# One layer of a hybrid encoder on one core: the mLSTM as one masked decay matrix per head, rotary by partition shuffles, query heads in pairs, gates as scans of rows

## The chip, the cores and the metric

One Trainium2 chip, one of its cores. The metric is the device time of one execution in microseconds, the median over several runs.

## The reference

One layer for a prompt of 256 tokens and a sample of 64 tokens, which share all weights; the kernel treats both as T = 320 columns. Everything reads xn = RMSNorm(x) through one input projection:

```python
# A: mLSTM, 8 heads of 128, chunk by chunk of 64 tokens
b = cumsum(lf);  logD = where(causal, b_t - b_s + ig_s, -inf)
m_t = max(b + m, max_s logD);  D = exp(logD - m_t);  inter = exp(b + m - m_t)
S = (q @ k.T) * D
h = (S @ v + inter * (C @ q)) / max(|sum(S) + inter * (n @ q)|, exp(-m_t))
C, n = decayed C, n + weighted outer products          # returned too
# B: 8 index heads of 64 with one key, relu, weighted sum, top-k keys per query;
#    softmax attention of 8 query heads (2 key/value heads of 128) over these keys;
#    q, k, index q, index k rotated in their first quarter of dimensions
# C: attention of 4 heads of 256 to 256 memory tokens
merged = sum_b sigmoid(G_b(xn)) * P_b(branch_b);  h = x + merged @ w_out
y = RMSNorm(h + ConvFFN(RMSNorm(h)))
```

## The kernel before, in words

Every product with weights is cut into **tiles** of 128 output features by 320 token columns (256 for the memory tokens). A tile has two **units** of eight k-blocks. In float32r, three products make one (high·high, low·high, high·low; `multiply`, L546 to L548), so a tile is 48 matmuls into one of two alternating PSUM banks `G`. SP loads a unit (512 KB) into one of four raw slots; ACT's `split` (L972) casts it to `w_hi`, DVE's `split` (L1333) subtracts that into `w_lo`, two units ahead of PE. After a tile ACT or DVE reads its bank, and PE may do a **stage** of small fp32 work into the six banks `M`: transposes by the identity (`turn`, L559) and products (`mm`, L562). The order on each engine is written out by hand in program order; the engines are tied by semaphores alone.

The order of the stages is C (4 heads of 6 tiles), B (10 tiles), A (8 heads of 4 tiles q, k, v, o), Q (8 query tiles), then gates and branches, output projection, FFN. What the change touches:

- **B and head 0 of A.** B's tiles are v, v, the gates i and f, the index key with the index weights, four of index queries, two of keys. For the rotary PE multiplies by a rotation matrix (the `mm` on `rin`, and `q_rotate` in Q) and DVE does three passes (`rope`, L1466). The gates are turned to tokens on rows; PE forms the chunks' sums and rows by products with constants (`decay_rows`, L783), DVE makes the decay matrix [5 chunks, 8 heads, 64], and the running maximum goes from chunk to chunk, with a product that broadcasts each chunk's last row (PE waits `g_mb`). Then the index scores (`logits`, L767): one product per head and query block, two banks in turn with ACT's relu (PE waits `i_relu`).
- **A.** During head h's four tiles PE does the four stages of head h−1: `a_scores` (L725), `a_outer` (L736), `a_values` (L747), `a_hT` (L760). DVE's `a_decay`, `a_recur` (L1533: five steps of the state C in series), `a_combine`, `a_gate` stand between. POOL copies `a_next` to `a_current` for each head.
- **Q.** A loop over four pairs of query tiles: after a pair's first tile `q_scores` (L840) of the pair before, after the second `q_probsT` (L848), `q_rotate`, `q_values` (L858). DVE's `q_softmax` (L1700) stands as a whole ahead of the pair's second `split`. The last pair's stages follow the first three gate tiles.

Of the kernel before, what the change touches and what calls it, by code (L numbers as in the profile page):

```python
# [65 lines left out]
U_A, T_A = U_B + 20, T_B + 10  # L66
# [7 lines left out]


C_ID, C_CAUS, C_CUM, C_LAST, C_ONE = 0, 128, 192, 256, 384
C_R128, C_R64, C_DUP, C_RDUP = 512, 640, 768, 896
C_COS128, C_SIN128, C_COS64, C_SIN64 = (1024 + n * T for n in range(4))
C_ADM = 1024 + 4 * T
CW = C_ADM + 2 * TP  # L80


def shape_tables():
# [4 lines left out]
    i = np.arange(CH)  # L88
    c[:CH, C_CAUS:C_CAUS + CH] = np.where(i[None, :] <= i[:, None], 0.0, NEG)
    c[:CH, C_CUM:C_CUM + CH] = i[:, None] <= i[None, :]  # L90
    c[CH - 1, C_LAST:C_LAST + P] = 1.0
    c[:, C_ONE:C_ONE + P] = 1.0

    def rotation(d):
        r = np.zeros((d, d), np.float32)
        half = d // 8
        for m in range(half):
            r[m + half, m] = -1.0
            r[m, m + half] = 1.0
        return r  # L100
    c[:, C_R128:C_R128 + P] = rotation(128)
    for o in (0, 64):
        c[o:o + 64, C_R64 + o:C_R64 + o + 64] = rotation(64)
    for o in (0, 64):
        c[:64, C_DUP + o:C_DUP + o + 64] = np.eye(64)
        c[:64, C_RDUP + o:C_RDUP + o + 64] = rotation(64)
    pos = np.arange(T).astype(np.float32)
    for d, oc, os in ((128, C_COS128, C_SIN128), (64, C_COS64, C_SIN64)):
        r, half = d // 4, d // 8
        inv = np.float32(500000.0) ** (-np.arange(half, dtype=np.float32) * np.float32(2.0) / np.float32(r))  # L110
        ang = pos[:, None] * inv.astype(np.float32)[None, :]
        for p in range(P):
            q = p % d
            c[p, oc:oc + T] = np.cos(ang[:, q % half]) if q < r else 1.0
            c[p, os:os + T] = np.sin(ang[:, q % half]) if q < r else 0.0
    for t in range(2):
        q = t * P + np.arange(P)
        end = (q // CH + 1) * CH
        c[:, C_ADM + t * TP:C_ADM + (t + 1) * TP] = np.where(np.arange(TP)[None, :] < end[:, None], 0.0, NEG)
# [27 lines left out]
class Place:  # L147


    def __init__(self, unit, tile):  # L150
        self.lap, self.pair = unit, tile

    def slot(self, j):
        return j % RING

    def loads(self, j):
        return (self.lap + j // RING) * 16 + 16

    def free(self, j):
        return self.lap * RING + (j + 1)  # L160

    def through(self, j):
        return self.lap * RING + (j + 1 + RING)

    def split(self, j):
        return self.lap * RING + (j + 1)

    def bank_free(self, t):
        return self.pair + (t // 2 + 1)

    def bank_read(self, t):
        return self.pair + (t // 2 + 2)


def place(unit, tile, i=0, units=0, tiles=0):

    assert unit % RING == 0 and units % RING == 0 and tile % 2 == 0 and tiles % 2 == 0
    return Place(i * (units // RING) + unit // RING, i * (tiles // 2) + tile // 2)


def layer(nc, a, o):

    with ExitStack() as ctx:
# [42 lines left out]
        bias16 = small("if_bias", [1])  # L226
        nout = small("n_out", [2, MH])
        nst = small("n_state", [MH])
        mst = small("m_state", [MH])
# [11 lines left out]
        mrow = pro("m_state_row", [MH])  # L241
# [42 lines left out]
        msk = wb("mask_bias", [2 * TP + SS])  # L284

        bcs = wb("b_cumsum", [NCH, MH])
        inter = wb("inter", [NCH, MH])
        wexp = wb("w_s", [NCH, MH])
        enm = wb("exp_neg_m", [NCH, MH])
        dec = wb("decay", [NCH, MH])  # L290
        mnew = wb("m_new", [NCH, MH])
        rb = Region(R_BB, R_K)
        Dm = rb("decay_matrix", [NCH, MH, CH])
# [3 lines left out]
        rl = rb("relu", [2, SS])  # L297
        ra = Region(R_BA, R_BB)
        vraw = ra("vT_raw", [2, T])
        kiw = ra("ikw_raw", [T])  # L300
        rin = ra("rope_in", [2, T])
        rtmp = ra("rope_tmp", [T])
        ifT = ra("if_T", [T])
        ckB = ra("cache_k", [2, 256])
        ckI = ra("cache_kidx", [2, 2, 64])
        kout = ra("k_tokens", [3, 256])
        kiout = ra("kidx_tokens", [3, 64])
        igf = ra("if_gates", [NCH, 16])
        g1 = ra("gate_tmp", [NCH, MH])
        g2 = ra("log_f", [NCH, MH])  # L310
        acs = ra("ig_minus_b", [NCH, MH])
        mxs = ra("row_max", [NCH, MH])
        mb = ra("m_and_b", [NCH, 2, MH])
        mint = ra("m_inter", [NCH, MH])
        blast = ra("b_last", [NCH, MH])
        diag = at("diag", R_W + 8 * T * 4, [NCH, MH, CH])
# [3 lines left out]
        a_nxt, a_cur = wa("a_next", [4, T]), wa("a_current", [4, T])  # L320
        q_c, k_c, v_c, s_c = (a_cur[:, n, :] for n in range(4))
        kw = wa("k_weighted", [NCH, P])
        vn = wa("v_tokens", [NCH, P])
        SD = wa("scores_decayed", [NCH, CH])
        sdT = wa("scoresT", [NCH, CH])
        Cst = wa("C_states", [7, P + 1])
        hn = wa("h_tokens", [NCH, P])
        ga = wa("h_gated", [T])
        cs = wa("C_state_head", [P])
        co = wa("C_out", [2, P])  # L330
        a_st = wa("a_stats", [2, 8])
        top8 = wa("top8", [3, 8])


        wq = Region(R_W, wc.off)
        q_raw = wq("q_raw", [2, T])
        q_nxt, q_cur = wq("q_next", [2, T]), wq("q_current", [2, T])
        v_cur = wq("v_current", [5, P])
        sp_ = wq("probs_prompt", [2, 2 * TP])
        ss_ = wq("probs_sample", [2, SS])  # L340
        pTp = wq("probsT_prompt", [2, 2 * TP])
# [1715 lines left out]
```

## Time and profile before

| | us |
|---|---|
| median of 3 runs | 2349.21 (2347.95 to 2351.01) |
| span of the profiled execution, first to last instruction | 2348.3 |
| PE busy | 2290.0 (98%), 15453 matmuls |
| DVE busy | 1297.3 (55%) |
| ACT busy | 923.8 (39%) |
| POOL busy | 95.4 (4%) |
| mean granted TensorE clock | 0.985 |

The profiled execution is known by its span; the runs' time stands 0.9 above it. Busy times of engines overlap and don't add up. PE's clock is granted in two levels, 1.2 and 2.4 GHz; 1.00 is the higher. In 40 slices of the span the page shows PE at 9 tenths or more nearly everywhere, and PEclk at 8 in slices 6 and 12, which lie in the stages that the change rewrites. B starts at 220.02, head 0 of A at 304, the steady heads at 379.22, Q at 644.14; the last stage of Q ends at 785.25.

### The profile page before, as it was taken

The page shows a single profiled execution, that of the slowest core. Times are in us where ns is not written, and L with a number is a line of the kernel's source. Part 1 is how long each engine was busy: PE and PEld are TensorE (multiplying, and loading weights), DVE is VectorE, ACT ScalarE, POOL GpSimd, SP SyncE. Part 2 cuts the span into 40 slices and gives each one's busy share as a digit, 9 for nine tenths or more (in the row PEclk, how much of TensorE's full clock was granted, in tenths as well). Part 3 has the DMA queues.
Part 4 walks back from the last instruction along what each step waited for, and adds up shares of the span by engine and source line. Part 5 has one row for each costly group of instructions (what it writes and reads, how often), then busy time and mean ns, then how long its engine had stood idle before and what let it go on. Part 6 is the DMA issues. An engine that isn't in the chain of part 4 may idle for free.

```text
span 2348.3 us, 43300 instructions
## 1 busy us (share of the span) xinstructions
PE 2290.0 (98%) x15453; PEld 2217.1 (94%) x15453; DVE 1297.3 (55%) x2089; ACT 923.8 (39%) x1534; POOL 95.4 (4%) x120
## 2 busy tenths in 40 slices
PE   6999989999999999999999999999999999999998
PEld 5999978999978999999999999999999999999998
DVE  5544465555555444444444556665666566656665
ACT  5443323223223423333323344443444444444454
POOL 4211000000001000000000000000000000000000
PEclk8999988999989999999999999999999999999999
DMA  6755432434323455555555545445544555454543
GB/s 184 228 169 143 125 97 79 126 104 120 108 80 89 119 156 148 146 143 154 144 155 176 153 133 161 143 135 164 148 143 137 164 145 145 139 163 143 148 136 122
DMA packets 617331, 329.75 MB, mean 140 GB/s; under 512 B 15407, under 2 KB 614055, under 8 KB 615971
## 3 DMA queue, kind: packets, MB, share of 16 engines
q1 hardware_dynamic: 614179, 316.04, 48.0%
q0 software_dynamic: 2784, 7.35, 1.0%
q10 hardware_dynamic: 288, 5.24, 0.6%
q8 instruction: 57, 0.93, 0.2%
q14 instruction: 23, 0.19, 0.0%
HBM read 319.27 MB, written 9.31 MB: 140 GB/s over the span
## 4 chain that ended last, share of the span: by engine, by line
PE 95%; DVE 2%; ACT 1%; DMA 1%; issue 1%; POOL 0%; DVEq 0%; ACTq 0%; POOLq 0%; SPq 0%
PE bank L546 29%; PE bank L547 29%; PE bank L548 29%; PE bank L562 6%; PE bank L559 3%; DMA hT<-xT_scratch 0%; DMA mem_tokens<-in_mem_prompt 0%; DVE w_lo L1333 0%; DVE x_scaled L1388 0%; ACT squares_unused L984 0%; ACT w_hi L972 0%; ACT conv L1249 0%; DVE decay_matrix L1667 0%; DVE conv L1825 0%; DVE conv L1827 0%
## 5 line engine op out<-in xcount | busy, mean ns | idle before, releaser
L546 PE MATMUL bank<-xn_hi,w_hi 128*128 128x320 f32 x3104 | 968.7, 312 | 6.9 <-issue 4.1
L547 PE MATMUL bank<-xn_lo,w_hi 128*128 128x320 f32 x3104 | 961.5, 310 | 0.3 <-issue 0.3
L548 PE MATMUL bank<-xn_hi,w_lo 128*128 128x320 f32 x3104 | 961.2, 310 | 0.0
L1333 DVE TENSOR_TENSOR w_lo<-w_raw,w_hi 128x1024 fp32r<-128x1024 f32 x628 | 749.9, 1232 | 278.1 <-ACT w_hi L972 271.6
L972 ACT CAST w_hi<-w_raw 128x1024 fp32r<-128x1024 f32 x628 | 634.0, 1049 | 189.9 <-PE bank L548 175.4
L546 PEld LDWEIGHTS bank<-xn_hi,w_hi 128*128 128x128 f32 x3104 | 582.8, 188 | 13.7 <-issue 9.2
L547 PEld LDWEIGHTS bank<-xn_lo,w_hi 128*128 128x128 f32 x3104 | 583.0, 188 | 2.4 <-issue 1.1
L548 PEld LDWEIGHTS bank<-xn_hi,w_lo 128*128 128x128 f32 x3104 | 582.5, 188 | 0.9
L546 PE MATMUL bank<-y_hi,w_hi 128*128 128x320 f32 x704 | 218.5, 310 | 5.5 <-DVE y_lo L1843 5.3
L548 PE MATMUL bank<-y_hi,w_lo 128*128 128x320 f32 x704 | 217.7, 309 | 0.0
L547 PE MATMUL bank<-y_lo,w_hi 128*128 128x320 f32 x704 | 217.7, 309 | 0.0
L1249 ACT ACTIVATE conv<-u_ext,conv_cols 128x322 f32<-128x322 f32 x88 | 58.1, 660 | 247.3 <-DVE u_ext L1821 247.3
L546 PEld LDWEIGHTS bank<-y_hi,w_hi 128*128 128x128 f32 x704 | 132.2, 188 | 7.6 <-issue 6.3
L547 PEld LDWEIGHTS bank<-y_lo,w_hi 128*128 128x128 f32 x704 | 132.2, 188 | 0.0
L548 PEld LDWEIGHTS bank<-y_hi,w_lo 128*128 128x128 f32 x704 | 132.2, 188 | 0.0
L1789 DVE TENSOR_TENSOR hT<-hT,bank 128x320 f32 (+1 forms) x80 | 39.0, 488 | 147.9 <-PE bank L548 140.9
L546 PE MATMUL bank<-branch_hi,w_hi 128*128 128x320 f32 x384 | 118.8, 309 | 0.0
L548 PE MATMUL bank<-branch_hi,w_lo 128*128 128x320 f32 x384 | 118.7, 309 | 0.0
L547 PE MATMUL bank<-branch_lo,w_hi 128*128 128x320 f32 x384 | 118.7, 309 | 0.0
L978 ACT ACTIVATE gate_tanh<-bank 128x320 f32<-128x320 f32 x48 | 21.0, 438 | 208.5 <-PE bank L548 208.5
L1825 DVE SCALAR_TENSOR_TENSOR conv<-u_ext,conv_cols,conv 128x322 f32<-128x322 f32 x88 | 48.9, 555 | 95.1 <-ACT conv L1249 95.1
L546 PE MATMUL bank<-merged_hi,w_hi 128*128 128x320 f32 x256 | 79.7, 311 | 2.2 <-DVE w_lo L1333 2.2
(368 smaller groups left out, 2237.3 us busy)
## 6 DMA issues: line engine op xcount, KB each, us to landing
w_raw<-in_w_in SPq DMA_DIRECT2D x208, 512.0 KB, 4.0
w_raw<-in_w_up SPq DMA_DIRECT2D x176, 512.0 KB, 4.5
w_raw<-in_w_down SPq DMA_DIRECT2D x64, 512.0 KB, 4.0
w_raw<-in_w_branch SPq DMA_DIRECT2D x48, 512.0 KB, 4.1
w_raw<-in_w_mem_kv SPq DMA_DIRECT2D x32, 512.0 KB, 5.0
w_raw<-in_w_out SPq DMA_DIRECT2D x32, 512.0 KB, 4.2
w_raw<-in_w_down SPq DMA_DIRECT2D x64, 192.0 KB, 3.4
xT_scratch<-xT ACTq DMA_DIRECT2D x1, 2560.0 KB, 10.7
```

Of the source, the lines that this page charges most:

```text
L546: pe.matmul(out, h, hi[:, k0 + k, 0:n], start=un == 0 and k == 0, stop=False)
L547: pe.matmul(out, h, lo[:, k0 + k, 0:n], start=False, stop=False)
L548: last = pe.matmul(out, l, hi[:, k0 + k, 0:n], start=False, stop=un == len(units) - 1 and k == nk - 1)
L559: return pe.transpose(out, in_, ident[0:in_.shape[0], 0:in_.shape[0]])
L562: return pe.matmul(out, lhsT, rhs, start=first, stop=last)
L972: act.copy(whi[:, pl.slot(j), :, :], raw[:, pl.slot(j), :, :]).then_inc(w_hi, 1)
L978: act.activation(out, G[t % 2][0:m, 0:n], func, scale=scale, **kw_).then_inc(bank_read[t % 2], 1)
L1249: act.activation(cbuf[:, e, 0:T + 2], ext[:, e, 2:E2], ACT.Identity, scale=ccols[:, 2, ds(col, 1)], bias=ccols[:, 3, ds(col, 1)]).then_inc ...
L1333: dve.tensor_tensor(wlo[:, pl.slot(j), :, :], raw[:, pl.slot(j), :, :], f32(whi[:, pl.slot(j), :, :]), ALU.subtract).then_inc(w_lo, 1)
L1789: dve.tensor_tensor(hT[:, k, :], hT[:, k, :], G[e][:, 0:T], ALU.add).then_inc(bank_read[e], 1)
L1825: own.did(dve.scalar_tensor_tensor(c, ext[:, e, 1:T + 3], ccols[:, 1, ds(col, 1)], c, ALU.mult, ALU.add))
```

## The change

It rewrites B, A and Q (220 to 785 us); tiles of C, gates, output and FFN keep their code, with `Place` generalised to units that don't start at a multiple of four.

- **B**: nine tiles. The gates, the index weights and the index key share one tile, filled by four small loads (16, 8 and 64 columns); SP waits for them (`bi_in`) before it goes on. The index queries' tiles compute only tokens from 64 on (`c0=CH`: 256 columns). The index products follow B's last four tiles, two heads each, key against query with keys on the free axis, relus on ACT, sums on DVE.
- **Gates** as rows, a head per partition: DVE scans [8 x 256] and [8 x 64] (`m_rows`, `b_rows`, `a_rows`, `x_rows`), gate functions on ACT; the rows are stored to DRAM, and POOL's `a_load` broadcasts a head's row to 64 partitions, twice.
- **Rotary**: DVE's `stream_shuffle` swaps partitions, POOL multiplies and adds (`rope`, L1931).
- **A**: the loop body is two heads with two sets of buffers. A head has one masked decay matrix [128 x 384 + 64]; the state enters as one product, and PE has two stages, behind a head's first and second tile. `a_outer`, `a_recur`, `a_hT` and the copy of `a_next` go; denominators are a product with ones, and DVE takes a reciprocal of [128 x 320].
- **Q**: eight tiles written out, heads in pairs with keys of the causal blocks only (384 of 512 columns); the scaling of the probabilities (`q_probs`) stands behind the next tile's `split` on DVE, `q_values` one tile later.

The core of the diff:

```diff
             pl = place(U_B, T_B)
+            for j in range(2):
...
+                sp.dma_start(raw[:, pl.slot(j), :, 0:16], w_in[:, k, O_IF:O_IF + 16]).then_inc(bi_in, 16)
+                sp.dma_start(raw[:, pl.slot(j), :, 16:24], w_in[:, k, O_IKW + 64:O_IKW + 72]).then_inc(bi_in, 16)
+            sp.wait_ge(bi_in, 64)
...
+            for t in range(9):
+                tile_x(pl, t, 2 * t, c0=CH if 1 <= t < 5 else 0)
...
+                if t >= 5:
+                    n = t - 5
+                    pe.wait_ge(b_rp, n + 2)
+                    if n:
+                        pe.wait_ge(i_relu, 4 * n)
+                    for e in range(2):
+                        q = 64 * e
+                        mm(M[3 + e][:, 0:P], iqT[q:q + 64, n, 0:P], ki2[q:q + 64, 0:P])
+                        mm(M[3 + e][:, P:KEYS], iqT[q:q + 64, n, P:TP], ki2[q:q + 64, 0:TP]).then_inc(i_lg, 1)
...
+            def a_values(h):
+                pe.wait_ge(a_sd, h + 1)
+                pe.wait_ge(a_vn, h + 1)
...
+            with pe.Fori(1, MH // 2) as i:
+                for e in range(2):
...
+                    for t in range(4):
+                        tile_x(pl, t, 2 * t)
+                        if t == 0:
...
+                            a_scores(before, i if e else i - 1, 1 - e)
+                        if t == 1:
+                            a_values(h)
...
+            def a_mask(i, e):
+                tri = K[:, C_TRI:C_TRI + P]
+                dve.wait_ge(a_de[e], i * 32 + 32)
+                dve.tensor_tensor(DE[:, e, 0:P], DE[:, e, 0:P], tri, ALU.add)
...
+            for t in range(AH):
+                i, e = t // 2, t % 2
+                split(pl, 2 * t, 2 * t + 1)
...
+                elif t >= 2 and e:
+                    q_probs(i - 1)
+                dve.wait_ge(bank_read[pl.bank(t)], pl.bank_read(t))
+                if t:
+                    dve.wait_ge(q_rope, t)
+                dve.stream_shuffle(qsh[0:32, 0:TP], qp[0:32, i % 2, e, :], SWAP128)
...
+                if t >= 2 and e == 0:
...
+                    q_masked(i - 1)
...
+            def rope(n, swapped, parts, cos, sin, done):
...
+                pool.tensor_tensor(swapped, swapped, sin, ALU.mult).then_inc(r_own, 1)
+                for x, lo, hi in parts:
+                    last = pool.tensor_tensor(x, x, cos[:, lo:hi], ALU.mult)
...
+                for half in range(2):
+                    pool.dma_start(DE[half * 64:half * 64 + 64, e, :],
+                                   gates[ds(h, 1), half, :].broadcast_to([64, XW])).then_inc(a_de[e], 16)
```

First place of the order: PE in the loop of A, the small work of one head between its tiles (`a_current` holds q, k, v; `C_states` the state per chunk; `scores_decayed` the masked scores). Before, of the four stages one repetition of each chunk's group:

```order
L562 MATMUL bank<-a_current 64x64
L559 MATMUL bank<-shape_consts,a_current 64x128 x2
...
L559 MATMUL bank<-shape_consts,scores_decayed 64x64
L562 MATMUL bank<-v_tokens,k_weighted 128x128
L562 MATMUL bank<-shape_consts,k_weighted 128x1
...
L562 MATMUL bank<-v_tokens,scoresT 64x128
L562 MATMUL bank<-C_states,a_current 64x128
L562 MATMUL bank<-C_states,a_current 64x1
...
L559 MATMUL bank<-shape_consts,C_states 128x128 x2
...
L559 MATMUL bank<-shape_consts,h_tokens 128x64 x5
```

and of the change the whole of a head:

```order
L551 MATMUL bank<-shape_consts,a_features 128x128 x2
L551 MATMUL bank<-shape_consts,a_features 64x128
L554 MATMUL bank<-a_features 128x256
L554 MATMUL bank<-a_features 128x128
L554 MATMUL bank<-a_features 64x64
...
L551 MATMUL bank<-shape_consts,C_state_head 128x128
...
L554 MATMUL bank<-scores_decayed,shape_consts 128x256
...
L554 MATMUL bank<-q_inter,n_state_columns 128x64
L554 MATMUL bank<-scores_decayed,v_tokens 128x256
...
L554 MATMUL bank<-k_weighted,v_tokens 128x128 x3
L554 MATMUL bank<-shape_consts,k_weighted 128x1 x3
```

The groups of each chunk are gone, and with them the transposes of the scores, of the states and of the result; what is left are wide products in two places instead of four.

Second place: DVE in Q, the softmax of one pair against the weight splits (`w_lo`). Before:

```order
L1704 SCALAR_TENSOR_TENSOR probs_prompt<-bank,mask_bias 128x512
L1705 SCALAR_TENSOR_TENSOR probs_sample<-bank,mask_bias 64x320
L1708 TENSOR_REDUCE q_stats<-probs_prompt 128x2
...
L1716 RECIPROCAL q_stats<-q_stats 128x2
L1717 RECIPROCAL q_stats<-q_stats 64x1
...
L1721 TENSOR_SCALAR probs_prompt<-probs_prompt,q_stats 128x256 x2
L1722 TENSOR_SCALAR probs_sample<-probs_sample,q_stats 64x320
...
L1333 TENSOR_TENSOR w_lo<-w_raw,w_hi 128x1024
```

and of the change:

```order
L1699 STREAM_SHUFFLE q_swapped<-q_prompt 32x256
L1700 STREAM_SHUFFLE q_swapped<-q_sample 32x64
...
L1662 SCALAR_TENSOR_TENSOR probs_prompt<-bank,mask_bias 128x384 x2
L1663 SCALAR_TENSOR_TENSOR probs_sample<-bank,mask_bias 128x320
L1665 TENSOR_REDUCE q_stats<-probs_prompt 128x2
...
L1311 TENSOR_TENSOR w_lo<-w_raw,w_hi 128x1024 x2
...
L1673 RECIPROCAL q_stats<-q_stats 128x5
L1678 TENSOR_SCALAR probs_prompt<-probs_prompt,q_stats 128x128
```

Masking and maxima stay ahead of the splits, with the shuffles of the tile's own rotary in front of them; the reciprocal and the scaling have moved behind two splits.

## Rows read from the trace of the kernel before

**Rows 1.** The page's chain that ended last: share of the span by engine

```profile
PE 95%; DVE 2%; ACT 1%; DMA 1%; issue 1%; POOL 0%; DVEq 0%; ACTq 0%; POOLq 0%; SPq 0%
```

**Rows 2.** Stage windows: us; PE, PEld, DVE, ACT, POOL busy; PEclk; DMA share; GB/s

```profile
220.02:379.22 159.20, 149.29 (x899) 130.99 (x898) 93.32 (x182) 53.85 (x91) 13.38 (x16) 0.91 0.37 101
379.22:644.14 264.92, 264.92 (x1878) 244.73 (x1877) 140.23 (x310) 76.42 (x123) 18.89 (x27) 1.00 0.42 113
644.14:785.25 141.11, 135.81 (x814) 118.20 (x812) 82.03 (x187) 49.88 (x117) 13.69 (x19) 0.95 0.33 89
```

**Rows 3.** PE's timeline, one head of A: start us, us, operation, shape

```profile
410.87 0.41 PE L546 MATMUL bank<-xn_hi,w_hi 128*128 128x320 f32 x1
...
421.03 0.39 PE L546 MATMUL bank<-xn_hi,w_hi 128*128 128x320 f32 x1
...
428.24 0.24 PE L559 MATMUL bank<-shape_consts,scores_decayed 64*64 64x64 f32 x1
...
449.75 0.41 PE L546 MATMUL bank<-xn_hi,w_hi 128*128 128x320 f32 x1
```

**Rows 4.** PE's timeline, a head of C: small stages between tiles

```profile
180.63 0.27 PE L559 MATMUL bank<-shape_consts,c_current 128*128 128x128 f32 x1
...
181.86 0.36 PE L546 MATMUL bank<-mem_hi,w_hi 128*128 128x256 f32 x1
...
187.70 1.89 PE L562 MATMUL bank<-c_current 128*128 128x256 f32 x8
...
190.52 0.39 PE L546 MATMUL bank<-mem_hi,w_hi 128*128 128x256 f32 x1
...
203.32 1.02 PE L562 MATMUL bank<-c_probsT,mem_v_tokens 128*128 128x256 f32 x4
...
205.86 0.39 PE L546 MATMUL bank<-xn_hi,w_hi 128*128 128x320 f32 x1
```

**Rows 5.** PE's timeline, a query pair: q_scores

```profile
737.02 1.03 PE L562 MATMUL bank<-kT_prompt,q_current 128*128 x4
...
740.40 0.42 PE L546 MATMUL bank<-xn_hi,w_hi 128*128 128x320 f32 x1
```

**Rows 6.** PE's timeline from 656 us, last head of A; a window inside it

```profile
656.22 0.21 PE L559 MATMUL bank<-shape_consts,scores_decayed 64*64 64x64 f32 x1 [1.66 <-DVE k_weighted L1528]
...
659.81 0.64 PE L546 MATMUL bank<-xn_hi,w_hi 128*128 128x320 f32 x1
...
669.00 0.43 PE L562 MATMUL bank<-v_tokens,scoresT 64*64 64x128 f32 x2
...
658.00:660.00 2.00, 2.00 (x12) 1.99 (x12) 0.08 (x1) 0.09 (x1) 0.00 (x0) 0.50 0.00 0
```

**Rows 7.** Groups by line and form: count, busy us, mean ns, idle before

```profile
L1704 DVE SCALAR_TENSOR_TENSOR probs_prompt<-bank,mask_bias 128x512 f32<-128x512 f32 x8 | 5.5, 682 | 18.6 <-PE bank L562 18.6
L1173 ACT ACTIVATE probs_prompt<-probs_prompt,q_stats 128x256 f32<-128x256 f32 x16 | 8.1, 505 | 17.1 <-DVE q_stats L1712 17.1
L972 ACT CAST w_hi<-w_raw 128x1024 fp32r<-128x1024 f32 x628 | 634.0, 1049 | 189.9 <-PE bank L548 175.4 <-DMA w_raw<-in_w_down 10.1 <-DMA w_raw<-in_w_mem_kv 3.4
L1348 DVE RECIPROCAL ffn_norm_var<-ffn_norm_var 128x320 f32<-128x320 f32 x1 | 2.2, 2153 | 0.5 <-ACT ffn_norm_var L988 0.5
L1941 POOL TENSOR_TENSOR xn_lo<-x_scaled,xn_hi 128x320 f32 x16 | 16.3, 1037 | 15.9 <-ACT xn_hi L997 15.8
```

**Rows 8.** DVE's and POOL's timelines around 220 us

```profile
214.59 2.36 DVE L1333 TENSOR_TENSOR w_lo<-w_raw,w_hi 128x1024 fp32r<-128x1024 f32 x2 [4.63 <-ACT w_hi L972]
...
220.63 3.73 DVE L1333 TENSOR_TENSOR w_lo<-w_raw,w_hi 128x1024 fp32r<-128x1024 f32 x2
...
220.89 2.39 POOL L1928 COPY c_current<-c_next 128x1664 f32<-128x1664 f32 x1 [12.63 <-DVE c_next L1338]
```

**Rows 9.** DMA issues: count, KB each, us from issue to landing

```profile
w_raw<-in_w_in SPq DMA_DIRECT2D x2, 64.0 KB, 2.2
```

More of the change, by code:

```diff
@@ L87, in shape_tables @@
     c[:, C_ID:C_ID + P] = np.eye(P)
[L88 to L91, printed above, removed]
     c[:, C_ONE:C_ONE + P] = 1.0
[L94 to L106, printed above, removed]
+    i = np.arange(P)
+    c[:, C_TRI:C_TRI + P] = np.where(i[:, None] <= i[None, :], 0.0, NEG)
     pos = np.arange(T).astype(np.float32)
@@ L825, in _ @@
-                if t == 3:
-                    for u in range(1, 3):
-                        for h in range(IH):
-                            logits(u, h)
-            a_stages = (a_scores, a_outer, a_values, a_hT)
-            pe.wait_ge(i_relu, 3 * IH)
-            pe.wait_ge(b_ko, 1)
-            pe.wait_ge(g_De, 1)
-            with pe.Fori(1, MH) as h:
-                pl = place(U_A, T_A, h, 8, 4)
-                for t in range(4):
-                    tile_x(pl, t, 2 * t)
-                    a_stages[t](h - 1)
+                    pe.wait_ge(b_v, 1)
@@ L859, in q_values @@
+                pe.wait_ge(q_pT, i + 1)
                 for e in range(2):
[L860 to L866 removed]
@@ L867, in q_values @@
-                    last.then_inc(q_pv, 1)
-            def q_rotate(pl, e):
-                pe.wait_ge(bank_read[e], pl.bank_read(e))
-                mm(M[2 * e][:, 0:T], K[:, C_R128:C_R128 + P], q_raw[:, e, :]).then_inc(q_rot, 1)
-            pl = place(U_Q, T_Q)
-            tile_x(pl, 0, 0)
-            a_scores(MH - 1)
-            a_outer(MH - 1)
-            tile_x(pl, 1, 2)
-            a_values(MH - 1)
-            a_hT(MH - 1)
-            for e in range(2):
-                q_rotate(pl, e)
@@ new lines, in a_head, with head @@
+                    if t == 2:
+                        a_mask(i, e)
+                        if before is not None:
+                            a_combine(before, 1 - e, stored)
+                    if t == 3 and before is not None:
+                        a_los(before)
+                    if rounds[t]:
+                        select(*rounds[t])
+            def head(i, e):
+                return place(U_A + 8 * e, T_A + 4 * e, i, 16, 8)
+            dve.wait_ge(c_out, 32 * CHD)
+            dve.wait_ge(i_acc, 6 * 4)
```

1267 lines of the change are left out of this document (616 added, 651 removed).

## The prediction

> **What bounds the kernel now.** I read the chain of waits first: 95% of the span lies on PE, so what PE executes, and the time for which PE stands, is the kernel [rows 1]. Then the windows of the three stages that the change rewrites: B with head 0 of A and the first tile of head 1 (220.02 to 379.22), the other heads (to 644.14), Q with the first gate tiles (to 785.25). The reader is to see three different limits [rows 2]. In the middle window PE is busy for all of its 264.92 us at full clock while DVE has 140.23 and ACT 76.42: there only fewer or shorter PE instructions count. In the first window PE stands for 9.9 us and in the last for 5.3, and the granted clock is 0.91 and 0.95: there waits count too, and what they cost in clock. The rest, before 220 and after 785, is the same in both kernels: it gives nothing.
>
> Then PE's own timeline. A weight tile between small stages takes 428.24 − 421.03 = 7.21 us for 48 matmuls of 320 columns; a head of A takes 449.75 − 410.87 = 38.88, so 38.88 − 4 × 7.21 = 10.0 us of a head is small work [rows 3]. A tile of 256 columns takes 187.70 − 181.86 = 5.84 [rows 4].
>
> **Prices of PE's small work** [rows 4]: twelve transposes take 1.23 us, 0.10 each; six fp32 products of 256 columns take 2.82, 0.47 each; four of 256 with four of 64 take 205.86 − 203.32 = 2.54, so 0.165 for 64 columns. On the line through both a product costs 0.27 at 128 columns, 0.57 at 320, 0.07 at one. By this the old head is 5 × (0.165 + 2 × 0.10) + 0.10 in scores, 5 × (0.10 + 0.27 + 0.07) in outer, 5 × (0.27 + 0.27 + 0.07) + 0.20 in values and 0.50 in its last transposes, 7.9 against the 10.0 measured: a factor of 1.27. The old q_scores, four products of 256 and two of 320, are 3.02 against 740.40 − 737.02 = 3.38, a factor of 1.12 [rows 5]. The old head is cut into pieces of 64 columns or tokens, q_scores is wide. The new stages are mostly wide, so I take 1.15, near the second, with 1.0 and 1.27 as ends.
>
> **Heads of A.** The change removes a_scores, a_outer, a_values and a_hT over five chunks. It adds a_scores behind a head's first tile (7 × 0.10 + 0.47 + 0.27 + 0.165 = 1.6) and a_values behind its second (2 × (0.47 + 0.27 + 0.165 + 0.165) + 3 × 0.27 + 3 × 0.07 = 3.2). 4.77 × 1.15 = 5.5 against 10.0: 4.55 less per head. Seven sets lie in the middle window: **−31.8**. Beside it, each head now loads its gate rows, broadcast to 64 partitions twice, on POOL's queue: a head ahead, some 34 us, where a 64 KB load lands in 2.2 [rows 9]; nothing. DVE and ACT do about 18 of these 34 us in my count with casts at 1.05, splits at 1.18 and the new reciprocal of 128x320 at 2.15 [rows 7, 8]; nothing while the next tile covers them.
>
> **B and head 0.** The change leaves nine tiles instead of ten, four of them at 256 columns; removes the rotation products, the diagonal products and the broadcasts of last rows, and with them PE's waits for DVE; and moves the index products up behind B's last four tiles. What remains: 5 × 7.21 + 4 × 5.84 = 59.4; the last head of C as before, 1.23 + 2.82 + 2.54 and six transposes at 0.10, 7.2 in all [rows 4]; index products 4 × (4 × 0.47 + 2 × 0.27 + 2 × 0.165) = 11.0 and 27 transposes 2.7, by 1.15 15.8; and 5 × 7.21 = 36.0 for head 0 and the next tile. Sum 118.4; 1.2, about a cast's time [rows 7], for the gate functions that ACT now does in front of a cast: 119.6 against 159.20: **−39.6**.
>
> Three unseen things lie beside this. The scans of [8 x 256] run at anything from 0.35 us (a one-input pass at the rate of 0.682 for 512 columns) to the reciprocal's 2.15 [rows 7]; ten behind tiles 2 and 3 of B have the time to tile 5, so nothing, or up to 10 us of DVE spread over three tiles at the high end, which delays w_lo by about 1 us. The rotaries move to POOL at three passes of 1.04 [rows 7], 3.1 us, one per tile of 5.84 to 7.21: hidden. SP waits once for four small weight loads before the next loads; at 2.2 us [rows 9] the two raw slots in reserve, a tile of 7.21, cover it.
>
> **Q.** Eight tiles and three gate tiles stay, 11 × 7.21 = 79.3. The last head costs 5.5. A pair costs q_scores 2 × (0.27 + 0.47) + 0.57 = 2.05, nine transposes 0.9, q_values 2 × (0.47 + 0.27) + 3 × 0.27 = 2.29; four pairs by 1.15 are 24.1. Sum 108.9. Now the wait: the probabilities are scaled behind the next split (second place shown of the order), so from q_scores to q_probsT run q_masked (0.51 + 0.51 + 0.43 by the 0.682 for 512 columns, the same columns again for the maxima: 3.1), five exps (0.505 for 256 columns, sums read out besides: 2.4), two casts 2.1, the second split 1.2 and the scalings 1.7 [rows 7, 8]: 10.5 us. PE has one tile, 7.21, for the first pair, and tile and q_values, 9.85, for the other three: stands of 3.3 + 3 × 0.7 = 5.4. Before, the whole softmax went ahead of the split. A stand costs clock as well: behind the idle 1.66 at 656.22 the small products ran to 659.81 at a granted 0.50, which is 1.2 GHz, and the next tile took 669.00 − 659.81 = 9.19 instead of 7.21 [rows 6]. One such loss, products and tile, about 3. 108.9 + 5.4 + 3 = 117.3 against 141.11: **−23.8**. The shuffles of 32 partitions stand ahead of q_masked on DVE: at the pass's rate 0.43, at the reciprocal's 2.15 [rows 7]; I take the low one, since it too is a copy, and keep +10 for six of them in a chain. The Trainium skill (VectorE: DVE Perf Modes, "The perf-mode tier table") has STREAM_SHUFFLE at about 2400 ns in its largest row, with no figure for 256 columns; no row of before shows one.
>
> **Sum.** −39.6 − 31.8 − 23.8 = −95.2 on a span of 2348.3: 2253.1; the median of the runs shown is 0.9 above that span, so **2254**. Low end: small work (72.9 us at factor 1) without the 0.15, −10.9, and no stand in Q, −8.4: 2235. High end: factor 1.27, +9; shuffles +10; POOL beside DVE, four times 1.37, +5.5; three further clock losses of about 2.5: 2286. 0.2%, 4.7 us, is about what a measurement of this kernel tells from no change.
>
> **Rivals.**
> (1) *POOL and DVE in each other's way.* A pair of splits took 2.36 us alone and 3.73 beside a POOL copy of 2.39 [rows 8], 1.37 more. If the whole rotary blocked the softmax chain in Q, 3.2 a tile over the four late tiles and one loss of clock would come to +15: **2269**. For it: the rotary of a tile starts right when q_masked may. Against: the row shows a part, not the whole 2.39. Chance 0.10. The Trainium skill (SBUF — State Buffer, "Who interferes with whom") calls the pair of ports an exclusive lock and lets a DVE instruction with two SBUF inputs contend with POOL's reads; the row agrees in direction, with 57% of the copy's time.
>
> (2) *A wait per head takes the place of the work removed.* a_values needs decays, casts and k_weighted of its own head one tile after a_scores. If that is late by 1.66, as k_weighted was at 656.22 [rows 6], each head pays 1.66, 0.8 for the small products at half clock (659.81 − 656.22 = 3.59 against 2.2 × 1.27) and 1.98 for the next tile, eight times 4.4 = 35.5: **2289**. Against: about 2.5 us of DVE and ACT work stand in a tile of 7.21, with two casts and splits ahead of it. Chance 0.10.
>
> (3) *Slower: the broadcast of gate rows comes late.* a_mask waits for it, in front of the weight splits on DVE. With −95 elsewhere the kernel turns slower once eight heads lose over 12 us each, so once the rows land some 46 us after issue (34 ahead, 12 late): beyond 2349, **2354** as its first value. Against: 2.2 for 64 KB [rows 9], though no row shows a broadcast read from DRAM into 64 partitions on POOL's queue. Chance 0.03.
>
> (4) *It does not do what it says:* casts, splits and loads set the pace, not PE, and only B's dropped tile, 7 us, counts: **2342**. Against: PE stands for none of the 264.92, with DMA at a share of 0.42 [rows 2]. Chance 0.03.
>
> **Chances.** The forecast has 0.74. Faster by over 0.2%: 0.74 + 0.10 + 0.10 and two thirds of (4), 0.96; within 0.2%: 0.01; slower: 0.03. The range 2235 to 2286 holds the forecast and (1), 0.84, and leaves out 0.16.
>
> **What would show it.** A head of A of 34.3 us with PE never standing; 256-column tiles of 5.84 behind B's first; no stand of PE between 300 and 340; in Q one stand of about 3 us before the first probability transposes, released by DVE's scalings, and small ones in the next pairs. Wrong would be: shuffles or scans above 1 us; a rotary on POOL above 4 us or splits stretched beside it; PE waiting for k_weighted or the decays once per head; a_mask waiting for the gate rows' DMA; a tile that waits for weights behind SP's wait in B.

## The result, and the profile after

The changed kernel takes 2253.41 us (median of 4 runs, 2251.94 to 2255.26) against 2348.58 in four runs of the kernel before beside it (2346.22 to 2351.01): a ratio of 0.9593, 95% interval 0.9579 to 0.9607. The forecast was 2254. The sum came out within a microsecond; the terms did not: they missed by up to 7 us in both directions, and that the misses cancel so closely is luck. Where they missed is what this section and the experiments are about.

The page of the changed kernel, busy times and the chain that ended last, against [rows 1]:

```profile
PE 2198.8 (98%) x14959; PEld 2165.7 (96%) x14959; DVE 1241.4 (55%) x1922; ACT 919.4 (41%) x1551; POOL 131.1 (6%) x181
...
PE 93%; DVE 3%; ACT 2%; issue 1%; DMA 1%; POOL 0%; DVEq 0%; ACTq 0%; POOLq 0%; SPq 0%
```

PE still ends nearly everything, but DVE has risen from 2% to 3% of the chain and ACT from 1% to 2%: a first sign that PE waits for them somewhere new. The stages now lie at other times. From B's first tile to the end of the first tile of head 1 it is 222.09 to 334.63, the other heads run to 570.86, Q to 685.64. The same windows of the changed kernel, columns as in [rows 2]:

```profile
222.09:334.63 112.54, 111.71 (x811) 106.50 (x810) 71.44 (x137) 48.02 (x84) 39.33 (x49) 1.00 0.57 155
334.63:570.86 236.23, 236.23 (x1585) 229.23 (x1583) 128.63 (x248) 81.72 (x147) 17.32 (x32) 1.00 0.54 137
570.86:685.64 114.78, 108.18 (x703) 103.79 (x701) 56.66 (x126) 46.83 (x115) 25.78 (x42) 0.97 0.39 105
```

| stretch | before | after | change | forecast |
|---|---|---|---|---|
| ahead of B | 220.02 | 222.09 | +2.1 | 0 |
| B and head 0 | 159.20 | 112.54 | −46.7 | −39.6 |
| heads of A | 264.92 | 236.23 | −28.7 | −31.8 |
| Q | 141.11 | 114.78 | −26.3 | −23.8 |
| behind Q (span's end) | 1563.05 | 1568.06 | +5.0 | 0 |
| span | 2348.3 | 2253.7 | −94.6 | −95.2 |

In B and head 0, PE stood for 9.91 us before (159.20 − 149.29) and stands for 0.83 now, and its granted clock rose from 0.91 to 1.00: 9.1 of the 46.7 are stands that went, the rest is less time in which PE is busy.

**Heads.** PE's timeline of one head of the changed kernel: a_scores at 334.63, a_values at 343.50, the next a_scores at 369.38.

```profile
334.63 0.49 PE L551 MATMUL bank<-shape_consts,a_features 128*128 128x128 f32 x3
...
343.50 1.18 PE L554 MATMUL bank<-scores_decayed,shape_consts 128*128 128x256 f32 x6
...
344.88 1.23 PE L554 MATMUL bank<-scores_decayed,v_tokens 128*128 128x256 f32 x6
...
346.31 1.08 PE L554 MATMUL bank<-k_weighted,v_tokens 128*128 128x128 f32 x6
347.32 0.92 PE L554 MATMUL bank<-shape_consts,k_weighted 128*128 128x1 f32 x6
348.17 0.41 PE L538 MATMUL bank<-xn_hi,w_hi 128*128 128x320 f32 x1
...
369.38 0.38 PE L551 MATMUL bank<-shape_consts,a_features 128*128 128x128 f32 x2
```

A head is 369.38 − 334.63 = 34.75 us against 38.88 [rows 3], forecast 34.3, and PE is busy for all 236.23 of the window: no wait has come in. The tiles were cheaper than forecast (7.04 where nothing stands between two of them), the small work dearer: a_values takes 348.17 − 343.50 = 4.67 instead of 3.6. Most of what was mis-sized is in the last products: three of a single column take 348.17 − 347.32 = 0.85, 0.28 each, where the straight line through 64 and 256 columns gave 0.07.

**Index products.** One tile's products in B, PE's timeline:

```profile
278.36 0.93 PE L554 MATMUL bank<-index_kT,index_qT 64*128 64x128 f32 x8
279.22 0.66 PE L554 MATMUL bank<-index_kT_cache,index_qT 64*64 64x256 f32 x4
279.70 0.29 PE L554 MATMUL bank<-index_kT,index_qT 64*64 64x64 f32 x4
279.92 0.42 PE L538 MATMUL bank<-xn_hi,w_hi 128*128 128x320 f32 x1
```

They take 279.92 − 278.36 = 1.56 us, and the forecast had 2.75 × 1.15 = 3.2. Four tiles make 6.4 of the 7.1 by which B came out better. The gate functions cost a little less than was forecast. ACT's and PE's timelines behind the second index tile:

```profile
241.78 0.46 ACT L1055 ACTIVATE gate_tmp<-gate_f 8x320 f32<-8x320 f32 x1
...
242.75 1.28 ACT L1059 ACT_TABLE_LOAD   x1
...
244.43 1.98 ACT L928 CAST w_hi<-w_raw 128x1024 fp32r<-128x1024 f32 x2
...
246.86 0.36 PE L538 MATMUL bank<-xn_hi,w_hi 128*128 128x256 f32 x1 [0.83 <-DVE w_lo L1311]
```

From 241.78 to 244.43 ACT works on the three gate functions (a table load of 1.28 in it) and only then casts; PE stands 0.83 for the w_lo made from that cast, where 1.2 was forecast.

**Q.** PE's timeline from the first transposes of probabilities (611.05) over the next tile (612.85) to the second pair:

```profile
611.05 1.51 PE L551 MATMUL bank<-shape_consts,probs_prompt 128*128 128x128 f32 x6 [3.42 <-DVE probs_sample L1679]
...
612.85 0.61 PE L538 MATMUL bank<-xn_hi,w_hi 128*128 128x320 f32 x1
...
621.82 0.38 PE L554 MATMUL bank<-kT_prompt,q_prompt 128*128 128x128 f32 x2
...
634.29 0.30 PE L551 MATMUL bank<-shape_consts,probs_prompt 128*128 128x128 f32 x1 [1.06 <-DVE probs_sample L1679]
```

and the engines behind it, from the end of the first pair's q_scores:

```profile
599.30 0.43 DVE L1699 STREAM_SHUFFLE q_swapped<-q_prompt 32x256 f32<-32x256 f32 x1
...
600.62 1.02 DVE L1662 SCALAR_TENSOR_TENSOR probs_prompt<-bank,mask_bias 128x384 f32<-128x384 f32 x2 [0.38 <-PE bank L554]
...
603.72 0.40 ACT L1142 ACTIVATE probs_prompt<-probs_prompt,q_stats 128x128 f32<-128x128 f32 x1 [4.46 <-DVE q_stats L1669]
...
606.04 1.98 ACT L928 CAST w_hi<-w_raw 128x1024 fp32r<-128x1024 f32 x2
...
607.10 2.36 DVE L1311 TENSOR_TENSOR w_lo<-w_raw,w_hi 128x1024 fp32r<-128x1024 f32 x2 [3.41 <-ACT w_hi L928]
...
609.60 1.01 DVE L1678 TENSOR_SCALAR probs_prompt<-probs_prompt,q_stats 128x128 f32<-128x128 f32 x4
610.52 0.38 DVE L1679 TENSOR_SCALAR probs_sample<-probs_sample,q_stats 128x320 f32<-128x320 f32 x1
```

The stands are 3.42 in the first pair and 1.06 in each of the other three (forecast 3.3 and 0.7), and all are released by DVE's scaling of the probabilities (L1679). The chain reads as forecast: masking and maxima to 603.69, exps to 606.04, two casts to 608.02, the splits to 609.46, scalings to 610.9. The shuffles take 0.43, the value taken. Behind the first stand the nine transposes took 1.80 instead of 0.93 in the next pairs, and the tile 621.82 − 612.85 = 8.97 instead of 7.12: 2.7 us, forecast 3. The products themselves came out 1 us per pair cheaper than forecast (19.9 at full clock for four pairs, where 24.1 was forecast), which pays for the longer stands.

**Behind Q.** Here nothing was changed, and here 5.0 us were lost. The window of the gate tiles, from Q's end to the third tile of the output projection, before:

```profile
785.25:1291.49 506.24, 501.15 (x3409) 499.85 (x3408) 217.16 (x241) 164.73 (x206) 0.00 (x0) 1.00 0.55 151
```

and in the changed kernel:

```profile
685.64:1198.93 513.29, 504.81 (x3410) 503.79 (x3409) 217.55 (x242) 164.71 (x207) 0.00 (x0) 0.99 0.54 149
```

This is 7.05 us more with the same DVE and ACT work. The gate tiles alone, to the first matmul of the output projection (1275.08 and 1183.76), lost 8.3. Part of it came back, because at the third tile of the output projection PE stood 2.17 before and 0.92 now, and the tile behind that stand took 8.69 before and 7.14 now; so 5.0 are left at the span's end. PE's timeline at the two jumps back of the loop of gate tiles, changed kernel:

```profile
919.45 0.41 PE L538 MATMUL bank<-xn_hi,w_hi 128*128 128x320 f32 x1 [1.23 <-issue]
...
922.99 0.30 PE L540 MATMUL bank<-xn_hi,w_lo 128*128 128x320 f32 x1 [2.54 <-issue]
...
1051.72 0.41 PE L538 MATMUL bank<-xn_hi,w_hi 128*128 128x320 f32 x1 [1.05 <-issue]
...
1055.44 0.43 PE L540 MATMUL bank<-xn_hi,w_lo 128*128 128x320 f32 x1 [2.73 <-issue]
```

At each jump PE stands twice: 1.23 and 1.05 at the jump, 2.54 and 2.73 five matmuls into the next tile. "issue" means that no engine and no DMA that the profile shows released it. The kernel before stood 1.37 and 1.20 at its jumps, then 0.32 once. The 48 matmuls behind the second stand, as many as a tile has, took 8.56 and 9.37 instead of 7.04, at a granted clock of 0.80 and 0.72. At the jumps of PE's other, shorter loops no "issue" stand of more than 0.2 is found.

### The profile page after: what moved, and what is told of

Read it like the earlier page. It is cut to its first block, busy times and chain, and to the rows that moved or that the text cites. A ratio compares the mean times of both kernels' runs of the same rounds, so it can differ in the third digit from the quotient of the medians.

```text
span 2253.7 us, 41938 instructions
## 1 busy us (share of the span) xinstructions
PE 2198.8 (98%) x14959; PEld 2165.7 (96%) x14959; DVE 1241.4 (55%) x1922; ACT 919.4 (41%) x1551; POOL 131.1 (6%) x181
## 3 DMA queue, kind: packets, MB, share of 16 engines
HBM read 322.29 MB, written 9.37 MB: 147 GB/s over the span
## 4 chain that ended last, share of the span: by engine, by line
PE 93%; DVE 3%; ACT 2%; issue 1%; DMA 1%; POOL 0%; DVEq 0%; ACTq 0%; POOLq 0%; SPq 0%
PE bank L538 30%; PE bank L540 29%; PE bank L539 29%; PE bank L554 4%; PE bank L551 2%; DVE w_lo L1311 1%; DMA mem_tokens<-in_mem_prompt 0%; DMA hT<-xT_scratch 0%; ACT w_hi L928 0%; ACT probs_prompt L1142 0%; DVE x_scaled L1366 0%; DVE probs_prompt L1662 0%; ACT squares_unused L941 0%; DVE probs_prompt L1678 0%; ACT conv L1227 0%
## 5 line engine op out<-in xcount | busy, mean ns | idle before, releaser
L538 PE MATMUL bank<-xn_hi,w_hi 128*128 128x320 f32 (+1 forms) x3088 | 959.3, 311 | 5.7 <-issue 2.9
L540 PE MATMUL bank<-xn_hi,w_lo 128*128 128x320 f32 (+1 forms) x3088 | 954.9, 309 | 5.3 <-issue 5.3
L539 PE MATMUL bank<-xn_lo,w_hi 128*128 128x320 f32 (+1 forms) x3088 | 954.9, 309 | 0.0
```

The costliest lines, as they stand in the source:

```text
L538: pe.matmul(out, h, hi[:, k0 + k, c0:n], start=un == 0 and k == 0, stop=False)
L539: pe.matmul(out, h, lo[:, k0 + k, c0:n], start=False, stop=False)
L540: last = pe.matmul(out, l, hi[:, k0 + k, c0:n], start=False, stop=un == len(units) - 1 and k == nk - 1)
```

## Experiments

Times are medians of four runs, with the ratio to seven runs of the kernel before beside them. The first eight kernels ran on one chip, where the kernel before took 2348.49 and 2349.13, the two with four and with forty transposes on another, where it took 2351.37.

**Is it the order of scaling and splits that makes PE stand in Q?** For the last pair, among the gate tiles, the same move is made.

```diff
             for t in range(AH):
                 i, e = t // 2, t % 2
+                if t >= 2 and e:
+                    q_probs(i - 1)
                 split(pl, 2 * t, 2 * t + 1)
                 if t == 0:
                     a_decay(MH - 1, 1)
-                elif t >= 2 and e:
-                    q_probs(i - 1)
```

> The changed kernel with DVE's scaling of the probabilities put ahead of the tile's two weight splits instead of behind them, for all four pairs. Theory (the prediction's: the chain masked scores, exps, casts, split, scalings sets PE's stands in Q): without casts and splits in it the chain is 3.1 + 2.4 + 1.8 = 7.3 us against a tile of 7.1, so the stands of 3.42 and 3 x 1.06 us shrink to under 1 us in the first pair and 0 in the others, the half-speed products behind the first stand (2.7 us) go too, and the time falls by 8 to 9 us to about 2245. Rival (the splits are what PE is short of): PE stands as long for w_lo as it stood for the probabilities, time within 2 us of 2253.

Measured 2245.46, ratio 0.9555 [0.9533, 0.9577]. Its window of Q, and the one stand left:

```profile
570.91:676.24 105.33, 105.11 (x704) 101.23 (x702) 57.94 (x126) 46.89 (x115) 28.89 (x42) 1.00 0.42 114
607.88 0.85 PE L551 MATMUL bank<-shape_consts,probs_prompt 128*128 128x128 f32 x6 [0.21 <-DVE probs_sample L1679]
```

The time fell by 8.0 us (by 6.7 against the second set of runs of the unaltered kernel, 2252.16). In Q, 114.78 has become 105.33, PE is busy for 105.11 of it, and the stand is 0.21 in the first pair and nothing in the others. Neither w_lo nor anything else took the place of the probabilities, so the rival falls: the two casts and splits were in the chain, and PE did not need them that early.

**Does PE alone set the pace of A?** The a_scores stage twice:

```diff
+                for s in range(3):
+                    n = P if s < 2 else TS
+                    turn(M[0][0:n, s * P:s * P + P], k[:, s * P:s * P + n])
...
+                turn(M[3][:, 0:P], cs[:, e, :])
                 turn(M[3][:, 0:P], cs[:, e, :]).then_inc(a_s0, 1)
```

> The changed kernel with PE's a_scores stage done twice per head (the same products into the same banks). Theory (PE alone sets the pace of A): each head grows by the stage's 1.74 us, eight heads by 13.9, time about 2267. Rival (casts, splits and loads set the pace and PE has slack that the trace does not show): less than 4 us more.

Measured 2258.82, ratio 0.9616 [0.9594, 0.9639], some 6 us above the unaltered kernel and so between theory and rival. The total misleads here; PE's timeline of this kernel, two a_scores of neighbouring heads and the two jumps back behind Q:

```profile
552.00 0.27 PE L551 MATMUL bank<-shape_consts,a_features 128*128 128x128 f32 x1
...
588.58 0.38 PE L551 MATMUL bank<-shape_consts,a_features 128*128 128x128 f32 x2
...
930.64 0.41 PE L538 MATMUL bank<-xn_hi,w_hi 128*128 128x320 f32 x1 [1.14 <-issue]
...
1058.72 0.41 PE L538 MATMUL bank<-xn_hi,w_hi 128*128 128x320 f32 x1 [1.10 <-issue]
```

A head has grown to 588.58 − 552.00 = 36.58, by 1.83 us: all of the added work is paid, 14.6 us for eight heads, as the theory has it. But at the jumps PE now stands only 1.14 and 1.10, the stand inside the tile is gone, and the tiles behind are at full speed: the stretch of gate tiles fell from 513.29 to 503.64. An edit in A had changed the time of a loop some 300 us later. What connects them is that PE's program became longer ahead of the loop, by 13 matmuls with their weight loads at each of the four places in the program that have this stage. This made the question of the fifth run and those behind it.

**Why are the index products so cheap?**

```diff
-                        q = 64 * e
+                        q = 0
...
-                        q, b = 64 * e, M[(5, 0)[e]]
+                        q, b = 0, M[(5, 0)[e]]
```

> The changed kernel with both heads of an index product taken from partitions 0 to 63 (before: one from 0 to 63, the other from 64 to 127); the second head's query rows are left out by this, so the selection of keys is not the reference's. Theory (two heads' products overlap on PE because they use different halves of its rows, which is why a tile's index products took 1.56 us where the prediction had 3.2): 1.56 becomes 2.7 to 3.1 and four tiles cost 4.5 to 6 us more, time about 2258. Rival (a product over 64 rows simply takes less time than one over 128): 1.56 stays, time within 1 us of 2253.

Measured 2256.39, ratio 0.9604 [0.9582, 0.9626]. The same stretch of PE as above, a tile's index products:

```profile
279.27 1.57 PE L554 MATMUL bank<-index_kT,index_qT 64*128 64x128 f32 x8
280.78 0.64 PE L554 MATMUL bank<-index_kT_cache,index_qT 64*64 64x256 f32 x2
...
281.37 0.59 PE L554 MATMUL bank<-index_kT_cache,index_qT 64*64 64x256 f32 x2
...
282.01 0.41 PE L538 MATMUL bank<-xn_hi,w_hi 128*128 128x320 f32 x1
```

282.01 − 279.27 = 2.74 instead of 1.56, the price that the line through the wide products gave (2.75). The first eight instructions take 1.5 instead of 0.9, and the small pairs now follow each other instead of sharing their time. The shapes are equal; only the half of the partitions differs. So products over partitions 0 to 63 and over 64 to 127 overlap on PE. Across the four tiles that is 4.7 us, most of B's surprise; the time rose by 3.0 (4.2 against 2252.16). The Trainium skill (TensorE: Matmul & The Clock Gate, "Why this matters for your kernels") states it for products over few partitions whose operands lie in different groups of rows; these runs agree, with 1.56 against 2.74.

**Do the narrower tiles of index queries give their full 1.2 us each?**

```diff
-                tile_x(pl, t, 2 * t, c0=CH if 1 <= t < 5 else 0)
+                tile_x(pl, t, 2 * t, c0=0)
```

> The changed kernel with the four index-query tiles computed for all 320 columns again instead of 256. Theory (PE sets the pace in B): each tile grows from 5.83 to 7.04 us, four by 4.8, time about 2258. Rival (weights or POOL's rotary set the pace of these tiles): PE waits less and the time stays within 1.5 us of 2253.

Measured 2256.64, ratio 0.9605 [0.9584, 0.9627]. The four tiles took 7.12 to 7.14 instead of 5.83, together 5.2 more, and the stand of 0.83 behind the gate functions went, since the longer tile covers ACT: the stretch is 4.3 longer. PE sets the pace here; the saving is real, less the stand it uncovers.

**The jumps back of the loop of gate tiles.** The unaltered kernel again:

> The changed kernel, unaltered, beside the next three. Theory (the 5 us by which the stretch behind Q is longer than before comes with where the loop of gate tiles now lies in PE's program, so it is there in every execution): again two stands of PE at each of the loop's two jumps back, 1.0 to 1.5 us and 2.2 to 2.8 us, time about 2253. Rival (chance of one execution): the stands or their lengths differ by more than a microsecond.

Measured 2252.16, ratio 0.9585 [0.9569, 0.9601]; the stands are 1.38 and 2.27, then 1.13 and 2.56, the second always five matmuls in, and the same five in the three kernels before that left PE's program as long as it was (the first, third and fourth). In these the first jump came up to 9.2 us earlier and 4.5 later than in the changed kernel, so it is the place in the program that counts and not the time. The 2.1 us ahead of B are not: B began at 220.20 in this execution and at 222.09 in the other, with a stand of 0.28 or 2.33 at PE's first weight tile.

```diff
+            for n in range(8):
+                turn(M[2][:, 0:P], K[:, C_ID:C_ID + P])
             with pe.Fori(1, KT // 4) as i:
                 merge_tiles(place(U_G, T_G, i, 36, 24), ())
```

> The changed kernel with eight transposes of the identity into an unused bank put on PE just ahead of the loop of gate tiles, about 0.8 us of work that nothing needs; it moves the loop's start along PE's program by the length of these instructions. Theory (the second stand at each jump, 2.54 and 2.73 us, waits for PE's next instructions and depends on how many of the loop's first instructions came with the jump): the second stands shrink or go, with them the slow tiles behind them (1.5 and 2.3 us), and in spite of 0.8 more work the time falls by up to 8 us, to 2245 to 2250. Rival (the jump itself costs this, wherever the loop lies): both stands stay, time 2254.

Measured 2242.10, ratio 0.9539 [0.9523, 0.9555]: eight transposes that nothing needs save 10 us. The window of the gate tiles in this kernel:

```profile
685.47:1187.43 501.96, 500.98 (x3418) 500.70 (x3417) 217.52 (x242) 164.97 (x207) 0.00 (x0) 1.00 0.55 152
```

501.96, against 513.29, with full clock; not only the second stand but also the one at the jump itself is gone. That is more than the theory had: with the loop in this place PE waits for nothing at its jumps.

```diff
-            with pe.Fori(1, KT // 4) as i:
+            for i in range(1, KT // 4):
                 merge_tiles(place(U_G, T_G, i, 36, 24), ())
```

> The changed kernel with PE's loop over the last three quarters of the gate tiles written out, all other engines as they are. Theory (the stands of 1.1 + 2.6 us at each jump back are PE's instructions coming late behind a jump, and straight code is read ahead): both pairs of stands and the slow tiles behind them go, 10 to 12 us, time about 2242. Rival (instructions come late in straight code too, or something else is late at the end of each quarter): under 3 us.

Measured 2240.37, ratio 0.9539 [0.9524, 0.9555]; the gate tiles take 501.54, without a stand at either place. Straight code and the shifted loop agree.

**By which rule does the place decide?** The unaltered kernel's second stand comes five matmuls, ten instructions, behind the loop's start. If the program comes in blocks, that is the distance to a border, and eight transposes (sixteen instructions) carry the start past it. A quarter of the gate tiles has 864 matmuls with a weight load each, 1728 instructions. The Trainium skill (Runtime: NRT & Kernel Launch, "Instruction fetch mechanics") has such blocks, of 256 instructions, and a stall where the target of a taken branch isn't in the current window of two pages, while it gives PE a memory of 2048 instructions. By two pages each of these jumps would stall, by 2048 instructions held none would; the runs show both, so what is measured decides. Two more shifts tell this from any shift doing it: four and forty transposes instead of eight.

> As the run with eight useless transposes ahead of the loop of gate tiles, with four. Each is a weight load and a matmul. In the unaltered kernel the second stand comes five matmuls, so ten instructions and a few for the jump, behind the loop's start. Theory (PE's program comes in blocks, and a jump waits for the block that it lands in and then for the next; eight transposes moved the start just past a block's border): eight instructions more leave the start ahead of that border, so both stands stay, the second after one matmul or two instead of five, time 2251 to 2255. Rival (any shift does it): no stand, as with eight, time about 2242.

Measured 2252.77, ratio 0.9581 [0.9565, 0.9597]. PE's timeline at the first jump:

```profile
916.91 0.41 PE L538 MATMUL bank<-xn_hi,w_hi 128*128 128x320 f32 x1 [1.41 <-issue]
920.09 0.43 PE L539 MATMUL bank<-xn_lo,w_hi 128*128 128x320 f32 x1 [2.77 <-issue]
```

Both stands are there, and the second now comes one matmul behind the start: four transposes, eight instructions, have brought the start four matmuls nearer to the border.

> The same with forty, 3.2 us more work than with eight. Theory (blocks, as above, and the loop stays resident as a whole only if it begins close behind a border): the start lies some 70 instructions into its block, the block must be fetched again at each jump and the next arrives in time, so one stand of 1.0 to 1.4 us at each jump and none inside the tile, time 2246 to 2250. Rival (any shift does it): no stand at all, and the time of the run with eight plus 3.2, about 2245.5; or stands as in the unaltered kernel, about 2256.

Measured 2249.42, ratio 0.9565 [0.9549, 0.9581]. The two jumps:

```profile
921.55 0.41 PE L538 MATMUL bank<-xn_hi,w_hi 128*128 128x320 f32 x1 [1.09 <-issue]
...
1049.55 0.41 PE L538 MATMUL bank<-xn_hi,w_hi 128*128 128x320 f32 x1 [1.01 <-issue]
```

One stand at each, 1.09 and 1.01, and none inside the tile, as the blocks have it; the run with a_scores twice, whose shift is longer still, shows the same. So the place of the second stand follows the distance to the next border, counted in matmuls over four placements (five, five minus four, and none for two), and the first was gone in one placement only, where the loop begins close behind a border. The second stand ends 3.2 to 3.7 us behind the first matmul of its pass in every execution that has one, in the kernel before too, where it came some twenty matmuls in and lasted only 0.32: the next block comes at about the same time, and what differs is how much work lies ahead of the border.

That blocks are fetched, and that the loop can stay resident, the DMA table of the pages shows: number of packets and MB of the queue whose count follows the edits of PE's program, in the unaltered kernel and in the one with eight transposes:

```profile
q8 instruction: 61, 1.00, 0.2%
...
q8 instruction: 43, 0.70, 0.1%
```

A packet has 1.00 MB / 61 = 16.4 KB. While PE goes straight through the first quarter and the loop's first pass, one follows another in 18.4 us on average (ten from 716.8 to 900.8), in which PE does some 125 matmuls with their weight loads: a block of about 250 instructions. The Trainium skill's 256 agree with that. Between 903 and 1168, where the loop's second and third pass lie, the unaltered kernel fetches 18 and the kernel with eight transposes none, so there the 1728 instructions stay resident over both jumps. With four and with forty transposes the page shows 61 again.

**The two edits together.**

> The changed kernel with DVE's scaling of the probabilities ahead of the splits and PE's loop of gate tiles written out, the two edits together. Theory (the two lie in different stretches and add): 8 and 11 us, time about 2234. Rival (what one saves the other needs): not below the better of the two alone.

Measured 2234.02, ratio 0.9509 [0.9493, 0.9525]: 6.4 us less than with the loop written out alone, 19 less than the change and 115 less than the kernel before. The two add, as the theory has it, and the rival falls.

## Why the prediction was right, and where it was not

- **What bounds it**: right. PE is busy for all of the heads' window, and doubling a stage there cost its whole time.
- **Heads** (−31.8, measured −28.7): the mechanism was right, the term "4.77 × 1.15 = 5.5" was not: the small work of a head is 6.4. It failed at "0.07 at one" column; such a product takes 0.28 (the kernel before has such products, but no row of them was read), and shapes of 64 to 128 columns stand above the line as well (1.38 and 1.43 for groups priced at 1.07). Tiles at 7.08 instead of 7.21 gave part of it back.
- **B and head 0** (−39.6, measured −46.7): the step "index products 4 × (...) = 11.0 ... by 1.15" failed. It took the price of products over 128 partitions for products over 64, and two heads in different halves overlap: 1.56 a tile. The gate functions' 1.2 was measured as a stand of 0.83. The scans, the rotary on POOL and SP's wait stayed hidden as forecast, though three of the prediction's signs of being wrong appeared in B: one scan of 256 columns took 1.11 (the other 0.66), one rotary on POOL took from 248.69 to 254.02, and splits were stretched beside POOL. No stand of PE came of them. A shuffle of 256 columns takes 0.43.
- **Q** (−23.8, measured −26.3): the chain and its four stands were right in place and releaser and nearly in size, and moving the scaling took them away. The term "four pairs by 1.15 are 24.1" was too dear: the pairs took 19.9, while the small work of a head took 1.35 times its line. One factor of 1.15 did not fit both: it was too small for the head's products, many of them of 1 to 128 columns, and too large for the pairs' wider ones. The shuffles took 0.22 to 0.51. The Trainium skill's figure of about 2400 ns for STREAM_SHUFFLE (VectorE: DVE Perf Modes, "The perf-mode tier table") is for 2048 elements, and these runs have no such row.
- **"The rest ... gives nothing"**: wrong, and the one step in which the reasoning failed and not a size. The code there is the same, but it lies elsewhere in PE's program, and the stretch behind Q was 5.0 us longer. The 2.1 ahead of B vary between executions.
- So 7.1 and 2.5 us better in B and Q stand against 3.1, 2.1 and 5.0 worse elsewhere. The mechanism and the range were right by reasoning; that the sum came within 1 us is luck, by errors that cancelled. The 0.9 added to the span was part of it: every run on record stands 1.5 to 1.7 us above its own span, and 0.9 compared a median with another execution.
- **Rivals.** POOL and DVE: they did get in each other's way in B. DVE's timeline for the two splits behind B's first tile, and POOL's for the rotary of the index key:

```profile
233.58 3.57 DVE L1311 TENSOR_TENSOR w_lo<-w_raw,w_hi 128x1024 fp32r<-128x1024 f32 x2 [0.78 <-ACT w_hi L928]
...
233.33 0.89 POOL L1934 TENSOR_TENSOR rope_swapped<-rope_swapped,shape_consts 128x320 f32<-128x320 f32 x1
234.16 1.90 POOL L1936 TENSOR_TENSOR index_kT<-index_kT,shape_consts 128x320 f32<-128x320 f32 x1
236.14 1.73 POOL L1940 TENSOR_TENSOR index_kT<-index_kT,rope_swapped 128x320 f32<-128x320 f32 x1
```

The splits took 1.75 and 1.90 instead of 1.18, and each ended about 1.1 behind the end of the POOL pass that was under way when it began; POOL's second and third pass took 1.90 and 1.73, and each ended 0.7 behind a split. They took turns. A multiplication on POOL that took 0.73 elsewhere in B took 3.67 beside two scans and two splits, which ran at full speed (1.19 and 1.21). So the Trainium skill's exclusive lock (SBUF — State Buffer, "Who interferes with whom") agrees with these rows in full, and the prediction read [rows 8] too mildly: the second of the two splits there began inside the copy (221.76) and ended 1.08 behind its end (223.28), so it stood for all of the copy's rest. In Q no stand came of it: masking, which reads one of its inputs from a PSUM bank, took 0.55 beside the rotary, against 0.51 forecast, and the rotary beside it ended at 603.04, ahead of the splits at 607.10. A wait per head: none. The gate rows' broadcast, the DMA issues of the changed kernel:

```profile
decays<-gate_scratch POOLq DMA_DIRECT2D x16, 208.0 KB, 5.5
```

5.5 us against the 34 there are. That the change would not do what it says fell with the second run.

What stays open: how close behind a border a loop must begin to stay resident (one placement within a few instructions of it did, one some 70 behind it did not), and what the stand of 1.0 to 1.5 us at the jump itself consists of; no run separates its parts.

## What to carry to other kernels

Price a stage from a row of the same shape, the operands' partitions included: a straight line through wide products missed one-column products by a factor of four and products over half the partitions by nearly two. When an engine is put into a chain, look at what stands ahead of it in program order on each engine of the chain; moving one call ahead of two splits was worth 6 to 9 us. And after any change to a program, read the "issue" stands at the jumps of long loops also where no code was changed, before a difference is put down to the edit: here, in a loop of 1728 instructions, they were worth 10 us, and the packets of the instruction queue tell whether a loop is fetched anew.

## What the runs showed of the hardware that was not expected

- Eight useless transposes ahead of a loop made the kernel 10 us faster (2252.16 to 2242.10), by moving the loop along PE's program; at its jumps PE had stood up to 3.8 us, and the clock granted behind was 0.72 to 0.80 over a tile.
- The stands at a jump follow the loop's place to within single matmuls: the second came five matmuls in, one matmul in with four transposes more, and not at all with eight or forty. PE's instructions come in packets of 16.4 KB, one for about 125 matmuls with their weight loads; with the loop in a good place 18 of 61 packets fall away.
- A DVE pass with two inputs in SBUF and a POOL pass took turns: two splits and two POOL passes each stood until the other engine's pass, begun before, had ended (1.75 and 1.90 instead of 1.18 for the splits).
- Two fp32 products over different halves of the partitions overlap on PE: 1.56 us against 2.74 for the same shapes in one half.
- The same stand of 3.42 us cost between 1.5 and 2.7 us of clock behind it (2.6 in a second execution of the same kernel), so its price is a range and not a figure.
